# Two 32-byte strips in the memory plan of a single-core two-block transformer kernel

## What is computed

```python
def swiglu(u, wg, wu, wd):
    return (jax.nn.silu(u @ wg) * (u @ wu)) @ wd
# first block, twice:   h += 0.5 * swiglu(rmsnorm(h)); h += mixer(rmsnorm(h)); h += 0.5 * swiglu(rmsnorm(h))
# second block, twice:  h += 0.5 * rms_norm(swiglu_2(rms_norm(h))); h += rms_norm(mixer(rms_norm(h))); same again
```

## The kernel before

| tensors | first byte, before | modulo 64, before |
|---|---|---|
| rawA, rawB, hiA, loA, hiB, loB, h, xs | 16512 (rawA0) to 98432 (xs) | 0 |
| xh, xl | 106624, 114816 | 0 |
| act_s, act_h, act_hh, act_hl | 123008 to 129152 | 0 |
| row_gain, cols, ident, ident_r, mask_r, ms, rstd | 131200 to 142592 | 0 |
| ms_eps, minus_half, act_warm | 142368 to 142880 | 32 |
| ckvh, ckvl, k_rope, cqh, cql | 142944 to 149088 | 32 |
| oh2, ol2 | 151136, 159328 | 32 |
| arena (all the mixers' work) | 167520 | 32 |

## Time and profile before

### The profile page before, as it was taken

One profiled execution on the slowest core, in us unless ns is written; L12 is line 12 of the kernel. 1 busy time (PEld: TensorE's weight loads), 2 busy tenths in 40 slices (PEclk: granted clock), 3 DMA queues, 4 the chain that ended last, 5 costly groups with the idle time before them and its releaser, 6 DMA issues.

```text
span 2008.1 us, 33785 instructions
## 1 busy us (share of the span) xinstructions
PE 1939.7 (97%) x13276; PEld 1794.8 (89%) x13276; DVE 1232.6 (61%) x1651; ACT 942.2 (47%) x1290; POOL 61.0 (3%) x98
## 2 busy tenths in 40 slices
PE   7999999999998989999999998999999999989998
PEld 7999899989997878999899997899989998878997
DVE  5556665665555646655655588666665655767555
ACT  5444544454445545444544456544454446445443
POOL 0000100000000000000100000100000000020000
PEclk9999999999999999999999999999999999999999
DMA  7545355445453125544544433554545553434452
GB/s 261 194 183 189 124 205 182 184 150 194 185 195 114 64 104 194 195 180 182 196 182 182 166 123 120 192 191 186 188 168 189 187 188 116 146 106 178 188 188 94
DMA packets 61119, 338.94 MB, mean 169 GB/s; under 512 B 6816, under 2 KB 7200, under 8 KB 32640
## 3 DMA queue, kind: packets, MB, share of 16 engines
q1 hardware_dynamic: 59040, 330.00, 44.4%
q0 software_dynamic: 2016, 8.06, 1.1%
HBM read 336.98 MB, written 1.05 MB: 168 GB/s over the span
## 4 chain that ended last, share of the span: by engine, by line
PE 87%; DVE 7%; ACT 4%; issue 1%; DMA 1%; POOL 0%; SPq 0%; DVEq 0%; ACTq 0%
PE X L1429 55%; PE Y L1429 31%; DVE arena L1251 2%; ACT hiA L526 1%; DVE loA L956 1%; DVE xl L983 1%; DMA rawA<-in_wa 1%; ACT xh L557 0%; PE Y L1780 0%; POOL rstd L431 0%; PE X L1463 0%; DVE h L1016 0%; ACT arena L687 0%; DVE xs L1009 0%; DVE arena L1395 0%
## 5 line engine op out<-in xcount | busy, mean ns | idle before, releaser
L1429 PE MATMUL X<-xh,hiA 128*128 128x256 f32 x2592 | 737.0, 284 | 5.8 <-DVE xl L983 4.9
L1429 PE MATMUL X<-xh,loA 128*128 128x256 f32 x2592 | 734.2, 283 | 0.0
L1429 PE MATMUL X<-xl,hiA 128*128 128x256 f32 x2592 | 734.2, 283 | 0.0
L956 DVE TENSOR_TENSOR loA<-rawA,hiA 128x2048 fp32r<-128x2048 f32 x221 | 506.4, 2291 | 295.0 <-ACT hiA L526 295.0
L1429 PEld LDWEIGHTS X<-xh,hiA 128*128 128x128 f32 x2592 | 497.6, 192 | 15.4 <-issue 4.3
L1429 PEld LDWEIGHTS X<-xl,hiA 128*128 128x128 f32 x2592 | 497.7, 192 | 5.5
L1429 PEld LDWEIGHTS X<-xh,loA 128*128 128x128 f32 x2592 | 497.6, 192 | 0.0
L526 ACT ACTIVATE hiA<-rawA 128x2048 fp32r<-128x2048 f32 (+1 forms) x233 | 424.1, 1821 | 82.6 <-PE Y L1429 46.8
L1429 PE MATMUL Y<-hiB,act_hh 128*128 128x512 f32 x704 | 276.6, 393 | 2.7 <-DVE act_hl L1069 2.7
L1429 PE MATMUL Y<-loB,act_hh 128*128 128x512 f32 x704 | 276.1, 392 | 0.0
L1429 PE MATMUL Y<-hiB,act_hl 128*128 128x512 f32 x704 | 274.4, 390 | 0.0
(11 more groups left out here) (234 smaller groups left out, 2069.3 us busy)
## 6 DMA issues: line engine op xcount, KB each, us to landing
rawA<-in_wa SPq DMA_DIRECT2D x221, 1024.0 KB, 5.5
rawB<-in_wb SPq DMA_DIRECT2D x181, 512.0 KB, 3.5
row_gain<-in_rows POOLq DMA_DIRECT2D x8, 512.0 KB, 7.5
arena<-in_gla POOLq DMA_DIRECT2D x1, 1280.0 KB, 10.3
h<-in_x SPq DMA_DIRECT2D x2, 512.0 KB, 4.4
rawA<-in_wa SPq DMA_DIRECT2D x2, 512.0 KB, 6.9
out<-h SPq DMA_DIRECT2D x2, 512.0 KB, 2.7
arena<-in_pool POOLq DMA_DIRECT2D x1, 768.0 KB, 8.8
```

The lines of the kernel that those rows point to most:

```text
L956: nc.vector.tensor_tensor(loA[p][:, :], rawA[p][:, :], hiA[p][:, :].bitcast(f32), ALU.subtract).then_inc(a_lo, 1)
L1429: return say(nc.tensor.matmul(*args, **kw))
```

## The change

Two tensors of 8 float32 (32 bytes per partition) that nothing reads or writes are put in the memory plan. The first moves `xh` and everything behind it by 32 bytes; the second moves `ckvh` and everything behind it by 32 more.

```diff
         h = sb("h", [P, TT, D])
         xs = sb("xs", [P, TT, D])
+        half_line = sb("half_line", [P, 8])
         xh = sb("xh", [P, KD, TOKENS], f32r)
         xl = sb("xl", [P, KD, TOKENS], f32r)
...
         act_warm = sb("act_warm", [P, 16])
+        half_line_2 = sb("half_line_2", [P, 8])
         ckvh = sb("ckvh", [P, TOKENS], f32r)
```

## The result

The changed kernel takes 1997.66 us (median of 4 runs, 1993.88 to 1998.26) against 2011.07 us of the kernel before (4 runs): the ratio is 0.9929, 95% interval 0.9917 to 0.9941. It is faster by 13.4 us. The forecast was 2011.5 us, no change, with a range that began at 2001.5.

A forecast was written before the change was run, and what follows sets the result against it. The prediction took TensorE, by matmul count times start-to-start distance, to bound the feed-forward layers. Its terms, -3.5 + 0.7 + 3.1 + 0.6 - 1.0 = -0.1 us, gave a median of 2011.5 us, range 2001.5 to 2019.5.

The forecast's parts named there:

- Part 1: Seven layers reading `xh`, 154 steps: the 48 matmuls 5.75 to 5.68 us, the 12 2.75 to 2.80; -3.5 us.
- Part 2: ffn2, 22 steps: moving operand stays at 32 modulo 64, stationary goes to 32, 2.77 to 2.80 us; +0.7 us.
- part 5: `xh`, `xl` moving outside these layers: 670 matmuls, each 1.7 ns cheaper; -1.0 us.
- Part 3: `xh`, `xl` stationary, 128x512, outside these layers: 528 matmuls, each 6.6 ns dearer; +3.1 us.
- Part 4: `xh`, `xl` stationary at 128x256, in pool and mla's query down-projection: 96 matmuls, each 6.6 ns dearer; +0.6 us.
- Part 6: VectorE, ScalarE, GpSimd and DMA: costed at nothing; transposes with `ident` moving within 0.8 us, in the range alone.
- A: TensorE distances depend on height in the partition or buffer pairs, so nothing changes: 2011.6 us; chance 0.20.
- B: In the layers the 48 gain and the 12 do not lose, steps 8.446 us: -9.3, 2002.3 us; chance 0.13.
- Rival C: Reads go by 128 bytes: the 12 lose, the 48 stay at 120 ns, steps 8.55 us: +13.7, 2025.3 us; chance 0.12.
- The two bounds: Moving blocks' mean 117.5 to 119.2 ns, -6 to +7 us; stationary 231 to 235 ns, -5 to +4 us.

The follow-up runs named there:

- oh32: Kernel before the change plus one 64-byte strip ahead of `ckvh`, moving `ckvh`, `cqh`, `oh2`, `ol2` and the arena only; 2006.75 us, a single run.
- all32: Kernel before the change plus one 32-byte strip ahead of `hiA`, moving weights and tokens alike; 2011.11 us beside 2011.02, a single run.
- map1: Separate TensorE-only kernel, not the reference's work: blocks of 48 or 24 matmuls with operand distances in 16-byte steps; 113.3 ns fastest, 120.0 ns at distance 0.
- xh96_oh64: Kernel before the change with three strips, putting `xh`, `xl` at 96 and `oh2`, `ol2` at 64 modulo 128; 2019.0 us, a single run.
- map2: Separate TensorE-only kernel: 12 by_tokens then 48 by_weights matmuls as in a feed-forward layer, at varied distances; steps 8.500 us (0 and 0) to 8.213 (0 and 112).

## Why the prediction was wrong

The step that failed is the price of a moving operand at 32, in parts 1 and 2 of the sum (part 5 uses it too). I took it from ffn2, as "48 take 5.68 us", because `oh2` and the new `xh` are both at 32 modulo 64. It measures 5.60. What `oh2` had before was a distance of 224 from `hiA`; the change puts both `oh2` and `xh` at a distance of 32. oh32 shows the two prices in the same layer, and all32 shows that for this shift the distance and not the place carries them.

- **Part 1, seven layers:** forecast a step of 8.477 us, measured 8.400: 154 x -0.077 = -11.9 us.
- **Part 2, ffn2:** forecast +0.7 us; measured 8.447 to 8.400, -1.0 us. That is -1.7 us against the sum.
- Together the mis-sized term is -13.6 us. With the forecast's -0.1 it makes -13.7; the medians moved by -13.4 us. The two profiled spans moved by 11.7, so the agreement is good to some 2 us and no better.
- **The 12 matmuls, part 1:** 2.80 us forecast and measured. **Part 3:** 233.3 ns forecast and measured, both halves of mla's output projection. This was luck. The price was carried over from `oh2` by the same wrong rule, from a distance of 224 to one of 32; it held because both of these cost 233 ns in map1, where 192 costs 229 and 240 costs 227.5.
- **Part 4:** forecast 6.6 ns dearer per matmul. In the traces the 128x256 matmuls with `xh` stationary, once settled in the second half of mla's query down-projection, went from 120.0 to 118.3 ns: cheaper. Over 96 matmuls that is -0.2 us instead of +0.6.
- **Parts 3 to 5 in all:** forecast +2.7 us; by the two traces the span fell by 11.7 us, of which the layers' steps are 154 x 0.100 + 22 x 0.047 = 16.4, so the rest lost 4.7. Two us of that are not in my parts. The granted clock was 0.989 over this span against 0.993 before, and matmuls ran inside the stretches at the lower level. One of them is in mla: after TensorE had been busy for 2.2 of the 4 us from 712 to 716, the granted clock was 0.50 from 716 to 720 us, the 1.2 GHz level, where the trace before has 1.00. The first nine matmuls of the output projection take 4.00 us there, and nine at 233.3 ns would take 2.10. That is 1.9 us lost in one place; such stretches lie elsewhere in each of the two traces, some to the other side, so the remainder can't be put down to the change.
- **Part 6:** VectorE's busy time went from 1232.6 to 1232.1 us, ScalarE's from 942.2 to 943.8. Costing them at nothing was right.

Of the rivals, A (height, or nothing at all) is refuted by the result; its aside, that the steady 120.0 ns "looks like two streams in a fixed relation", was the right hint, but I used it for the modulo. B (gain without loss) was near in sign but wrong in its mechanism: the 12 did get slower. Rival C named the doubt that mattered, that 32 need not act like 96 modulo 128, and I priced it in one direction alone: as a loss of the gain. Its limit for the sign is off as well: by my own terms 176 blocks of 48 at 118.8 ns, not 119.2, make +4 us. No row gave a bound of 5.68 us for the 48 from below; my interval of 117.5 to 119.2 ns was set around the one value I had seen, and the true 116.7 lay outside of it. The two bounds also don't add up to the 6 us that I wrote: as independent they make about 8. With hindsight, a range for a price seen at two places only could have reached as far below the lower one as the two differ: 118.3 - 1.7 = 116.6 ns. Over 7392 matmuls that is -12.6 us, which puts the lower end at about 1998.9 and, with the stationary bound, at 1998.0, just above the measured 1997.66. No run tests such a rule.

## What to carry to other kernels

Where a TensorE that never waits sets the time, look at where the moving and the stationary operand begin relative to each other, and try distances in steps of 16 bytes over 256: here the same 13276 matmuls took from 1966 to 2019 us by empty strips and the order of allocation alone. Measure the distances in a small kernel that enters each block as the real one does, since what ran before can decide between two paces; map2 came within 0.2% of the full kernels' steps at the four settings compared. A pair of tensors that differ in one property, such as an offset modulo 64, differs in others too; before carrying its price over, move both operands together, and each alone, and see which of these changes the time.

## What the runs showed of the hardware

- The distance from start to start of a 128x256 matmul with a new stationary operand each time was 113.3 to 120.8 ns by place at a granted clock of 1.00, for steps of 8 and 16 bytes, and up to 123.2 for steps of 4; for 128x512 it was 226.7 to 234.5 ns. The lowest values of the two shapes are the same per column, 0.443 ns.
- It follows the distance between the two operands modulo 256 bytes (the 32 distances of map1 repeat after 16), and not the place of either where both were moved by 32 (all32). In map1 pairs shifted by 32 to 256 bytes take a pace of their distance within 0.3 ns, and weights moved by 16 bytes are an exception that stays open.
- One distance can hold two paces, each stable over whole blocks: 117.8 and 113.6 ns at 192, 116.7 and 117.8 at 32 (map1). In map2 the two at 192 went with the distance of the 12 ahead; in xh96_oh64 they took turns behind the same 12. What selects the pace is open.
- The Trainium skill, "SBUF — State Buffer", section "Who interferes with whom", gives TensorE two independent read ports and says that it waits on nobody. These runs measure no port, but in map1, where no other engine works, the pace of one operand depends on where the other begins. What in the chip makes it so was not settled; that the reads of the two get in each other's way is the reading I would test next, and it is argued only.
